# Two more weight places, one row slot fewer, halved attention maps, and loads placed three blocks behind

## The chip, the cores and the metric

The kernel runs on one core of one Trainium2 chip. The metric is the device time of one execution in microseconds (us), lower is better. All numbers are fp32; a "block" of weights is 128 partitions x 2048 values, 1.05 MB.

## What is computed

A trunk of two layers over 256 tokens of width 1024. The part of the reference that matters here, cut to its core:

```python
def reference(x, p, ...):
    h = layer_norm(x, ln_in_g, ln_in_b)
    for i in range(DEPTH):                                   # 2 layers
        mix = token_mixers(h, w_in[i], w_out[i], ...)        # differential attention + indexed sparse attention
        h = layer_norm(ALPHA * h + mix, ln1_g[i], ln1_b[i])
        r = ALPHA * h + peer_ffn(h, peer_wq[i], peer_subkeys[i], peer_u[i], peer_v[i])
        gate = sigmoid(r @ ple_wg[i] + ple_bg[i])
        h = layer_norm(r + gate * (p[i] @ ple_wp[i]), ln2_g[i], ln2_b[i])

def peer_ffn(h, w_q, sub_keys, u_tab, v_tab):                # tables of 16384 experts x 1024
    q = (h @ w_q).reshape(T, 8, 2, 128)                      # 8 heads, 2 halves
    s = einsum('thcd,hckd->thck', q, sub_keys)
    s1, i1 = top_k(s[:, :, 0], 16); s2, i2 = top_k(s[:, :, 1], 16)
    best, pos = top_k((s1[..., :, None] + s2[..., None, :]).reshape(T, 8, 256), 16)
    eidx = take_along_axis(i1[..., :, None] * 128 + i2[..., None, :], pos)   # 8 x 16 experts a token
    act = gelu(einsum('thkd,td->thk', u_tab[eidx], h))
    return einsum('thk,thkd->td', softmax(best) * act, v_tab[eidx])
```

## The kernel before

**Work.** The tokens go in two tiles of 128. Each pair of layer and tile is a run, 0 to 3: runs 0 and 1 are the tiles of the first layer, 2 and 3 those of the second. A run has a *mix* part (projections, both attentions, output projection, first norm, the queries `pq`, the key scores `ps`, and the choice of 128 experts a token) and a *close* part (gate, embedding, second norm). For every run 128 gathers follow: gather k fetches for each of the 128 tokens one expert's row of u and v (2048 values, 1.05 MB in all) from HBM.

**Phases and pairs.** After a start-up the program has four phases. Phase k takes the 128 gathers of run k-1, two at a time, in 64 pairs, and between the pairs it does pieces ("parts") of the mix of run k and of the close of run k-2. Which part stands at which pair on TensorE (PE), ScalarE (ACT) and VectorE (DVE) is written out by hand in `START_*`, `FIRST_PLAN`, `PROJECT_PLAN`, `ATTEND_PLAN`, `CLOSE_PLAN` and their last-phase variants; `make_plan` lays them out. A pair is: two dot products on DVE (L1303, row times token), gelu and two diagonal matrices on ACT (L829, L832, L835), and 2 x 8 small matmuls on PE that add gate times v into the accumulator (L1663; L1658 in the last phase). I write (2,14) for pair 14 of phase 2. Parts named A, B, C with a group number are the choice of experts on DVE: A is the top 16 of each half, B the top 16 of the 256 sums, C the look-up of the indices; `A2b` is group 2, second head.

**Buffers and queues.** Rows land in a ring of `RING` slots. GpSimd (POOL) issues gather k when PE has finished gather k - `RING` (L622, semaphore `slot_done`). The first gathers also wait for some slots that hold weight blocks during the start-up (`EARLY`, `EARLY_SLOTS`). Weight blocks go through a `store` of `PLACES` places. SyncE (SP) issues the loads strictly in the order in which PE uses them (L571), and each load waits for the last use of the block that its place held before. `KEPT_BLOCKS` are blocks that the second tile of a layer needs too: they stay in their places from the first tile's use to the second's. The place of each load is chosen when the program is built, in `count_uses`:

```python
at = min((a for a in range(PLACES) if run is not CLOSE[2] or a not in HELD_LATE), key=lambda a: free[a])
```

that is, the place whose block was done with longest ago.

## Time and profile before

| | |
|---|---|
| median of 3 runs | 1598.83 us (1597.42 to 1599.74) |
| the profiled execution's own time | 1597.55 us, span 1595.8 us |
| busy share of the span | PE 76%, DVE 66%, ACT 42%, POOL 36% |
| moved by DMA | 648.45 MB, mean 406 GB/s |
| of these the gathers (software queue) | 536.90 MB |
| of these the SP and ACT loads | 109.76 MB and 0.34 MB |

The profiled execution is 1.3 us under the median. The rates in GB/s are read against the rate that the DMA engines hold when they have work all the time, which the windows show as 421.

### The profile page before, as it was taken

How to read it: one execution, taken by the hardware profiler on the slowest of the kernel's cores; microseconds unless marked ns; L12 is line 12 of the kernel's file. 1: busy time of each engine (PE TensorE's matmuls, PEld its weight loads, DVE VectorE, ACT ScalarE, POOL GpSimd, SP SyncE). 2: the span in 40 equal slices, each digit the busy share in tenths (PEclk: the TensorE clock that was granted, in tenths of full speed). 3: DMA queues.
4: the chain of work that ended last, by engine and by line, in shares of the span. 5: the costliest groups of instructions: out<-in, count | busy, mean ns of one | idle time of the engine just before them, and what ended most of it. 6: DMA issues, size and time to landing. Idle time of an engine off the chain costs nothing.

```text
span 1595.8 us, 22703 instructions
## 1 busy us (share of the span) xinstructions
PE 1213.1 (76%) x8234; PEld 603.9 (38%) x8234; DVE 1045.3 (66%) x2636; ACT 668.6 (42%) x2027; POOL 580.9 (36%) x518
## 2 busy tenths in 40 slices
PE   9999868787868689786895977978798768444556
PEld 9686423333532266231551335524255223000112
DVE  3467997745778664654688684575578958644555
ACT  2323445723344435363344532536344534323444
POOL 0013443443333323343344332334443434544441
PEclk9999989898888899797997978999899876555557
DMA  9869999999999999999999999999999999999996
GB/s 384 360 250 396 396 421 420 421 421 420 421 420 421 417 396 421 421 420 421 421 421 421 421 417 370 420 421 420 422 420 419 420 421 420 422 421 421 421 421 248
DMA packets 91344, 648.45 MB, mean 406 GB/s; under 512 B 10144, under 2 KB 11616, under 8 KB 13152
## 3 DMA queue, kind: packets, MB, share of 16 engines
q0 software_dynamic: 74016, 536.90, 81.3%
q1 hardware_dynamic: 16704, 109.76, 16.8%
q8 instruction: 65, 1.06, 0.3%
q10 hardware_dynamic: 512, 0.34, 0.1%
q14 instruction: 47, 0.39, 0.1%
HBM read 645.91 MB, written 1.05 MB: 405 GB/s over the span
## 4 chain that ended last, share of the span: by engine, by line
DMA 45%; PE 30%; DVE 14%; ACT 7%; issue 3%; POOL 2%; SPq 0%; ACTq 0%; DVEq 0%; POOLq 0%
DMA rows<-uv_dram,rows_of 39%; PE bank L1343 10%; PE acc L1663 7%; DVE rows L1303 7%; PE bank L1361 5%; DMA store<-wmix_dram 4%; POOL rows L622 2%; ACT dg L835 1%; PE acc L1658 1%; ACT L832 1%; ACT ex L748 1%; PE bank L1614 1%; DMA rows<-wmix_dram 1%; ACT gel L832 1%; DMA store<-wclose_dram 1%
## 5 line engine op out<-in xcount | busy, mean ns | idle before, releaser
L622 POOL DMA_INDIRECT rows<-uv_dram,rows_of x510 | 576.7, 1131 | 985.9 <-PE acc L1663 661.3
L1303 DVE CUSTOM_DVE_ANT_0 rows<-rows,hb 128x1024 f32<-128x1024 f32 x384 | 463.9, 1224 | 313.1 <-DMA rows<-uv_dram,rows_of 310.6
L1663 PE MATMUL acc<-rows,dg 64*64 64x512 f32 x3072 | 453.1, 701 | 198.0 <-ACT dg L835 196.2
L832 ACT ACTIVATE gel<-dots 128x1 f32<-128x1 f32 x512 | 102.7, 201 | 630.1 <-DVE dots L1303 628.7
L1663 PEld LDWEIGHTS acc<-rows,dg 64*64 64x64 f32 x3072 | 102.0, 145 | 459.7 <-ACT dg L835 369.3
L1343 PE MATMUL bank<-xT,store 128*128 128x128 f32 x1888 | 235.1, 286 | 15.7 <-DMA store<-wmix_dram 10.4
L1343 PEld LDWEIGHTS bank<-xT,store 128*128 128x128 f32 x1888 | 225.5, 200 | 55.5 <-issue 41.9
L1303 DVE CUSTOM_DVE_ANT_0 rows<-rows,store 128x1024 f32<-128x1024 f32 x128 | 155.5, 1224 | 119.3 <-DMA rows<-uv_dram,rows_of 118.7
L1658 PE MATMUL acc<-rows,dg 128*32 128x256 f32 x1024 | 119.7, 565 | 133.3 <-ACT dg L835 132.8
L835 ACT ACTIVATE dg<-dg,gel 128x64 f32<-128x64 f32 (+1 forms) x512 | 174.7, 341 | 48.4 <-ACT gel L832 1.5
L1361 PE MATMUL bank<-store,xT 128*128 128x512 f32 x352 | 166.3, 618 | 17.2 <-DMA store<-wmix_dram 14.4
L829 ACT ACTIVATE dg<-fixed,g_of 128x64 f32<-128x64 f32 (+1 forms) x512 | 143.5, 329 | 1.4 <-ACT probsT L648 0.3
L1658 PEld LDWEIGHTS acc<-rows,dg 128*32 128x32 f32 x1024 | 25.9, 132 | 222.9 <-ACT dg L835 212.5
L1361 PEld LDWEIGHTS bank<-store,xT 128*128 128x128 f32 x352 | 66.3, 196 | 110.4 <-issue 94.0
L832 ACT ACT_TABLE_LOAD x51 | 65.4, 1283 | 0.9
L648 ACT ACTIVATE probsT<-bank 128x512 f32<-128x512 f32 (+1 forms) x59 | 30.7, 545 | 42.4 <-PE bank L1343 32.6
L1303 DVE DVE_READ_ACCUMULATOR2_ANT dots<- 128x1 f32 x512 | 42.1, 82 | 0.0
L648 ACT ACTIVATE qT<-bank 128x512 f32<-128x512 f32 (+1 forms) x18 | 9.9, 550 | 59.7 <-PE bank L1343 49.8
L1489 PE MATMUL bank<-prm,fixed 64*128 64x256 f32 x96 | 27.5, 433 | 0.0
L777 ACT ACT_TABLE_LOAD x20 | 25.7, 1283 | 0.4
L1253 DVE TENSOR_TENSOR ex<-ex,i16f 128x512 f32<-128x512 f32 (+1 forms) x38 | 22.6, 594 | 1.3
L1256 DVE TENSOR_REDUCE sel<-ex 128x32 f32<-128x512 f32 (+1 forms) x38 | 22.4, 588 | 1.3
(230 smaller groups left out, 1016.2 us busy)
## 6 DMA issues: line engine op xcount, KB each, us to landing
store<-wmix_dram SPq DMA_DIRECT2D x78, 1024.0 KB, 9.7
store<-wclose_dram SPq DMA_DIRECT2D x15, 1024.0 KB, 10.4
rows<-uv_dram,rows_of POOLq DMA_INDIRECT x510, 16.0
rows<-wmix_dram SPq DMA_DIRECT2D x5, 1024.0 KB, 14.8
rows<-prm_dram SPq DMA_DIRECT2D x2, 1024.0 KB, 19.1
store<-wmix_dram SPq DMA_DIRECT2D x2, 512.0 KB, 9.1
res<-x_dram SPq DMA_DIRECT2D x1, 512.0 KB, 3.7
rows<-wmix_dram SPq DMA_DIRECT2D x1, 512.0 KB, 7.4
```

What stands on the lines that cost most here:

```text
L622: pool.indirect_dma_start(out=rows[:, slot, :], out_offset=None, in_=uv_d[phase // TILES], in_offset=bass.IndirectOffsetOnAxis(ap=rows_of[ ...
L648: ins = A(out, src, func)
L777: A(gexp[:, 0:gs], gexp[:, 0:gs], ACT.Exp).then_inc(gexp_ready, 1)
L829: A(dg[:, s + j, 0:w], one, ACT.Identity, scale=g_of[:, phase % 2, col:col + 1]).then_inc(diag_ready, 1)
L832: A(gel[:, s + j:s + j + 1], dots[:, s + j:s + j + 1], ACT.Gelu).then_inc(gelu_done, 1)
L835: A(dg[:, s + j, 0:w], dg[:, s + j, 0:w], ACT.Identity, scale=gel[:, s + j:s + j + 1]).then_inc(dg_ready, 1)
L1303: V.tensor_tensor_reduce(out=rows[:, s, 0:D], in0=rows[:, s, 0:D], in1=tokens, scale=1.0, scalar=0.0, op0=ALU.mult, op1=ALU.add, accum_out ...
L1343: ins = MM(bk[:, T * at:T * at + T], w[:, T * c:T * c + T], src[:, c, :], start=(c == 0), stop=(c == KC - 1))
L1361: ins = MM(bk[:], xT[:, 2 * q + c, :], w[:, 512 * c:512 * c + 512], start=(q == 0 and c == 0 and extra is None), stop=(q == 3 and c == 1), ...
L1489: ins = MM(bk[:, QCOLS * j:QCOLS * j + QCOLS], chooser(first + i // 2, 2 * (i % 2) + j), prm[:], start=True, stop=True)
L1658: ins = MM(quarters(acc, c)[BT * k:BT * k + BT, :], dg[:, s, 0:BT], rows[:, s, D + 256 * k:D + 256 * k + 256], start=False, stop=False, sk ...
L1663: ins = MM(acc[HT * j:HT * j + HT, 512 * r:512 * r + 512], dg[at, s, :], rows[at, s, D + 512 * j:D + 512 * j + 512], start=False, stop=Fal ...
```

## The change

- The store grows from 10 to 12 places, the ring shrinks from 8 to 7 slots.
- A ninth block, that of `pq0a`, joins `KEPT_BLOCKS`: runs 1 and 3 don't load it again. SP issues 99 block loads in place of 101.
- A load takes the place freed third last before its use (`AHEAD = 3`), not the one freed longest ago; run 0 keeps the old rule.
- Four, not six, of run 0's blocks sit in row slots at the start (`EARLY`); `dk0` and `dk1` sit in the store and are lent to run 1 (`LENT`), which now uses them in phase 1.
- To pay for the store, `ex` (attention maps, key scores) and `probsT` (transposed maps, queries) are halved to 4 maps and 8 blocks (`HELD = 4`). For the second tile the second half of the heads therefore waits until the first is done: `exps1` for `wts0`, `sexp1` for `spt0`, `spt1` for `spv0`, `ps3` and `ps4` for the C step of the groups two before.
- The plans are written out anew around it; parts behind the mix move some pairs later.

```diff
-PLACES = 10
+PLACES = 12
+HELD = 4
-RING = 8
+RING = 7
...
 FIRST_PLAN = [
-    ("pq2a", 0, None, None), ("pq2b", 1, 2, None), ("pq3a", 2, None, None), ("ps2", 3, 4, None), ("pq3b", 4, 5, None),
-    ("pq4a", 5, None, None), ("ps3", 6, 7, None), ("pq4b", 7, 8, None), ("ps4", 9, 10, None),
+    ("pq2a", 1, None, None), ("pq2b", 2, 3, None), ("ps2", 4, 5, None), ("pq3a", 5, None, None), ("pq3b", 7, 8, None),
+    ("ps3", 8, 9, None), ("pq4a", 10, None, None), ("pq4b", 11, 12, None), ("ps4", 13, 14, None),
...
 SINGLY_FIRST = [
-    ("T", 9, 10, None), ("par", 9, 10, None), ("sq0", 11, None, None), ("iw", 13, 14, None), ("sq1", 13, 14, None),
+    ("dk0", 3, None, None), ("dk1", 9, 10, None), ("T", 13, 14, None), ("par", 13, 14, None), ("sq0", 15, None, None),
+    ("iw", 17, 18, None), ("sq1", 17, 18, None),
 ]
+def behind_mix(row):
+    part, *pairs = row
+    late = [p for p in pairs if p is not None]
+    if part[:2] in ("sp", "gb", "mT", "mi", "me") or min(late) < 37:
+        return row
+    return (part, *(None if p is None else p + (2 if p < 54 else 1 if p < 62 else 0) for p in pairs))
...
 def attend_first(p):
-    return p + max(0, min(6, 6 - (p - 50) // 3))
+    return p + max(0, min(8, 8 - (p - 50) // 3))
...
-EARLY = [(U_IQ, U_IQ + 1), (U_IK,)] + [tuple(units_of(part)) for part in ("dq0", "dq1", "dk0", "dk1")]
-EARLY_SLOTS = (3, 2, 4, 5, 6, 7)
-KEPT_BLOCKS = [(U_SK, U_SK + 1)] + [tuple(units_of(part)) for part in ("pq1a", "pq2a", "pq2b", "pq3a", "pq3b", "pq4a", "pq4b")]
+EARLY = [(U_IQ, U_IQ + 1), (U_IK,)] + [tuple(units_of(part)) for part in ("dq0", "dq1")]
+EARLY_SLOTS = (3, 2, 4, 5)
+LENT = [tuple(units_of(part)) for part in ("dk0", "dk1")]
+KEPT_BLOCKS = [(U_SK, U_SK + 1)] + [tuple(units_of(part)) for part in ("pq0a", "pq1a", "pq2a", "pq2b", "pq3a", "pq3b", "pq4a", "pq4b")]
+AHEAD = 3
...
-                at = min((a for a in range(PLACES) if run is not CLOSE[2] or a not in HELD_LATE), key=lambda a: free[a])
-                assert free[at] < i
+                if run is CLOSE[2] and not late:
+                    late = tuple(sorted(range(PLACES), key=lambda a: free[a])[:3])
+                open_to = sorted((a for a in range(PLACES) if free[a] < i and a not in late), key=lambda a: free[a])
+                at = open_to[0] if run is MIX[0] else open_to[max(0, len(open_to) - AHEAD)]
...
                 if part in ("exps0", "exps1"):
                     half = int(part[4])
                     act.wait_ge(dmax_ready, n + n // 2 + 1 + half * tile)
+                    if half and tile:
+                        act.wait_ge(dw_ready, DIFF_HEADS * n + DIFF_HEADS // 2)
...
-                    take(run, part[:3], lists[:, 2 * h0:2 * h0 + 2 * nh, :].rearrange("p c t -> p (c t)"), slice(0, 2 * nh * T))
+                    if part in ("ps3", "ps4"):
+                        act.wait_ge(*((rows_picked, len(GROUPS) * n + g - 1) if n < LAST else (chosen_ready, g - 1)))
+                    take(run, part[:3], lists[:, halves_of(h0, nh), :].rearrange("p c t -> p (c t)"), slice(0, 2 * nh * T))
```

Where the change moves instructions, at three places.

PE, from the last matmuls of the start-up into phase 1. `bank<-res,rows` are run 1's projections from blocks in row slots (`res` holds its transposed tokens), `acc<-rows,dg` the two gathers of a pair. Before:

```order
L1639 MATMUL acc<-hb,fixed 64x512 x4
L1527 MATMUL bank<-store,probsT 128x128 x2
L1343 MATMUL bank<-res,rows 128x128 x48
L1343 MATMUL bank<-xT,store 128x128 x16
L1663 MATMUL acc<-rows,dg 64x512 x8
```

Now:

```order
L1682 MATMUL acc<-hb,fixed 64x512 x4
L1570 MATMUL bank<-store,probsT 128x128 x2
L1383 MATMUL bank<-res,rows 128x128 x16
L1706 MATMUL acc<-rows,dg 64x512 x8
L1383 MATMUL bank<-xT,store 128x128 x16
L1706 MATMUL acc<-rows,dg 64x512 x8
L1383 MATMUL bank<-xT,store 128x128 x16
L1706 MATMUL acc<-rows,dg 64x512 x8
L1383 MATMUL bank<-res,store 128x128 x16
```

In rows as printed x16 is one block. Two of three blocks of run 1 (`dk0`, `dk1`) and the block of `pq2a` have moved from ahead of the first pair to behind it; the first stands at pair 3 now.

PE again, from the end of phase 1 into phase 2 (`acc<-hb,fixed` is `init`, which opens the accumulator of phase 2; `bank<-store,probsT` is a `ps` part). Before:

```order
L1527 MATMUL bank<-store,probsT 128x128 x4
L1663 MATMUL acc<-rows,dg 64x512 x40
L1639 MATMUL acc<-hb,fixed 64x512 x4
L1333 MATMUL bank<-fixed,res 128x128 x8
```

Now:

```order
L1383 MATMUL bank<-xT,store 128x128 x16
L1706 MATMUL acc<-rows,dg 64x512 x16
L1682 MATMUL acc<-hb,fixed 64x512 x4
L1570 MATMUL bank<-store,probsT 128x128 x4
L1373 MATMUL bank<-fixed,res 128x128 x8
```

`ps4` of run 1 stood five pairs ahead of the turn and stands behind it now; the choice of run 1's experts is packed more closely around the turn.

SP, the loads of the last two runs (`wclose` blocks, then `wmix` blocks of run 3). Before:

```order
L571 DMA store<-wclose_dram 128x2048 x4
L571 DMA store<-wmix_dram 128x2048
L571 DMA store<-wmix_dram 128x1024
L571 DMA store<-wmix_dram 128x2048 x17
L592 DMA store<-fixed_dram 128x664
```

Now:

```order
L600 DMA store<-wclose_dram 128x2048 x4
L600 DMA store<-wmix_dram 128x2048
L600 DMA store<-wmix_dram 128x1024
L600 DMA store<-wmix_dram 128x2048 x16
L621 DMA store<-fixed_dram 128x664
```

One full block fewer; the same holds for run 1. What each load waits for follows from `count_uses` and the plans. For the loads around the projections of runs 2 and 3 it gives (used at, part; waits for the last use at, part):

```
run 3 before: (3,14) dq0 <- (3,13) idx   (3,15) dq1 <- (3,13) idx   (3,16) dk0 <- (3,14) dq0   (3,17) dk1 <- (3,15) dq1
run 3 now:    (3,14) dq0 <- (3,5) g1b    (3,15) dq1 <- (3,13) idx   (3,16) dk0 <- (3,13) idx   (3,17) dk1 <- (3,14) dq0
run 2 before: (2,14) dq0 <- (1,56) ps3   (2,14) dq1 <- (1,58) pq4a  (2,15) dk0 <- (1,58) pq4b  (2,15) dk1 <- (2,1) ple
run 2 now:    (2,14) dq0 <- (2,5) g1b    (2,14) dq1 <- (2,13) idx   (2,15) dk0 <- (2,13) idx   (2,15) dk1 <- (2,14) dq0
run 1 before: (1,11) sq0 <- mix1b of the start-up   (1,13) sq1 <- pq0a of the start-up   (1,22) sk0 <- (1,11) sq0
run 1 now:    (1,15) sq0 <- mix1b of the start-up   (1,17) sq1 <- (1,3) dk0              (1,24) sk0 <- (1,9) dk1
```

By the same count the loads up to pair 13 of phase 2 are 55 before and 47 now; one of the eight is the load that is dropped, so seven move to behind that pair.

## Rows read from the trace of the kernel before

**Rows 1.** The page: what DMA moved.

```profile
DMA packets 91344, 648.45 MB, mean 406 GB/s; under 512 B 10144, under 2 KB 11616, under 8 KB 13152
```

**Rows 2.** Windows: busy of each engine, granted clock, DMA share, GB/s.

```profile
70.00:108.00 38.00, 36.56 (x234) 27.47 (x233) 15.30 (x54) 6.74 (x14) 4.20 (x5) 1.00 0.53 184
108.00:140.00 32.00, 32.00 (x279) 26.06 (x278) 21.74 (x75) 13.90 (x37) 11.12 (x12) 1.00 0.98 385
160.00:170.00 10.00, 8.65 (x69) 4.11 (x71) 9.72 (x19) 6.77 (x17) 5.99 (x4) 1.00 0.90 320
200.00:540.00 340.00, 258.16 (x1552) 116.08 (x1552) 238.56 (x614) 151.16 (x446) 125.42 (x113) 0.89 1.01 421
540.00:580.00 40.00, 25.58 (x148) 10.72 (x140) 38.80 (x102) 17.06 (x48) 11.91 (x11) 0.71 1.00 398
...
940.00:970.00 30.00, 18.44 (x124) 11.88 (x121) 25.66 (x61) 12.16 (x37) 8.51 (x7) 0.73 1.01 412
970.00:975.00 5.00, 5.00 (x37) 4.04 (x37) 2.47 (x4) 0.00 (x0) 0.00 (x0) 0.73 0.34 121
```

**Rows 3.** DMA issues: KB of one, median us from issue to landing.

```profile
store<-wmix_dram SPq DMA_DIRECT2D x78, 1024.0 KB, 9.7
...
rows<-uv_dram,rows_of POOLq DMA_INDIRECT x510, 16.0
```

**Rows 4.** Timeline, 100 to 126 us: start, us, engine, line; POOL, then PE.

```profile
102.58 1.07 POOL L622 DMA_INDIRECT rows<-uv_dram,rows_of  x1 [102.13 <-DVE rows_of L1177]
...
115.66 0.93 POOL L622 DMA_INDIRECT rows<-uv_dram,rows_of  x1 [2.64 <-PE bank L1343]
...
124.36 0.94 POOL L622 DMA_INDIRECT rows<-uv_dram,rows_of  x1 [4.20 <-PE acc L1663]
...
108.08 10.88 PE L1343 MATMUL bank<-res,rows 128*128 128x128 f32 x96
...
122.46 1.95 PE L1663 MATMUL acc<-rows,dg 64*64 64x512 f32 x16
```

**Rows 5.** Timeline, 955 to 976 us, PE, SP and POOL.

```profile
957.47 1.95 PE L1663 MATMUL acc<-rows,dg 64*64 64x512 f32 x16
967.40 6.31 PE L1343 MATMUL bank<-xT,store 128*128 128x128 f32 x32 [7.98 <-DMA store<-wmix_dram]
...
957.57 16.50 SPq L571 DMA_DIRECT2D store<-wmix_dram  x3
...
975.04 0.94 POOL L622 DMA_INDIRECT rows<-uv_dram,rows_of  x1 [12.96 <-PE acc L1663]
```

**Rows 6.** Gathers by window (145:165, 540:575, 1380:1480), us to landing.

```profile
DMA to landing us min/median/max: 7.7/8.8/9.4
...
DMA to landing us min/median/max: 7.8/9.9/16.6
...
DMA to landing us min/median/max: 16.0/16.5/17.7
```

**Rows 7.** DVE timeline: an A, a B and a C step, each to what follows it.

```profile
545.65 0.48 DVE L893 MAX8 v<-ex 128x8 f32<-128x128 f32 x2
...
548.75 1.28 DVE L857 BATCH_NORM_STATS2 stats<-res 128x6 f32<-128x512 f32 x2
...
554.17 0.42 DVE L1239 TENSOR_TENSOR sc<-v 128x256 f32<-128x256 f32 x1
...
557.14 1.23 DVE L1303 CUSTOM_DVE_ANT_0 rows<-rows,hb 128x1024 f32<-128x1024 f32 x1
...
566.04 0.18 DVE L1260 TENSOR_TENSOR gexp<-best 128x32 f32<-128x32 f32 x1
...
568.84 1.22 DVE L1303 CUSTOM_DVE_ANT_0 rows<-rows,hb 128x1024 f32<-128x1024 f32 x1
```

**Rows 8.** POOL timeline, the last gathers (L622) and half gathers (L633).

```profile
1561.85 1.20 POOL L622 DMA_INDIRECT rows<-uv_dram,rows_of  x1 [1.28 <-PE acc L1658]
1569.38 1.12 POOL L633 DMA_INDIRECT rows<-uv_dram,late_of  x1 [6.34 <-PE acc L1658]
```

More of the change, by code:

```diff
@@ L159, in loads_of @@
     if run is MIX[1]:
-        blocks = [b for b in blocks if b not in EARLY]
+        blocks = [b for b in blocks if b not in EARLY + LENT]
     return [b for b in blocks if not (run.stage == "mix" and run.tile and b in KEPT_BLOCKS)]
@@ L222 @@
               (f"zgate{_d}", 0, 0, None), (f"zblend{_d}", None, None, 0), (f"zsum{_d}", 0, None, None), (f"znorm{_d}", None, 0, 0)]
-START_PE = ("wake T idx dq0 dq1 dk0 dk1 iw ds0 ix sq0 sq1 dv0 dv1 dpt sk0 dpv sk1 ss0 sv0 sv1 mT0 mix0a spt0 spt1 mix1p spv mix1a mT1 "
-            "T1+ mix0b mix1b idxa+ h1T pq0a ps0 idxb+ dq0+ pq1a init ps1 dq1+ dk0+ dk1+").split()
+START_PE = ("wake T idx dq0 dq1 dk0 dk1 iw ds0 ix sq0 sq1 dv0 dv1 dpt sk0 dpv sk1 ss0 sv0 sv1 mT0 mix0a spt0 spt1 mix1p spv0 spv1 mix1a mT1 "
+            "T1+ mix0b mix1b idxa+ h1T pq0a ps0 idxb+ dq0+ pq1a init ps1 dq1+").split()
 START_ACT = ("embed0 T par idx dq1 dk1 iw ix exps0 exps1 sq1 dv1 dpt dpv sk1 rms sexp0 sexp1 sv1 mT0 embed1 spt0 spt1 mT1 T1+ n1a "
@@ L272, in make_plan @@
         plan[e][0] = [(0, p.rstrip("+"), MIX[p[-1] == "+"]) for p in parts]
-    plan["ACT"][1].append((1, "dk1", MIX[1]))
     def lay(phase, rows, run, moved=int):
@@ L350, in count_uses @@
     last, end = last_reads(), sum(1 for _ in pe_order())
-    uses, free = [0] * PLACES, [-1] * PLACES
+    uses, free, late = [0] * PLACES, [-1] * PLACES, ()
     for i, (part, run) in enumerate(pe_order()):
@@ L746, in part_of @@
                     act.wait_ge(smax_ready, n + n // 2 + 1 + half * tile)
+                    if half and tile:
+                        act.wait_ge(*full_at(run, "spt1"))
                     for i in range(4 * half, 4 * half + 4):
-                        A(ex[:, i, 0:run.keys], sc[:, i, 0:run.keys], ACT.Exp, bias=snmx[:, i:i + 1], scale=SCALE,
+                        A(map_of(run, i), sc[:, i, 0:run.keys], ACT.Exp, bias=snmx[:, i:i + 1], scale=SCALE,
                           accum_out=sden[:, i:i + 1]).then_inc(sexp_ready, 1)
@@ L751, in part_of @@
                     for name in banks_of(run, part):
[L752 removed]
+                        take(run, name, quarter(probsT, int(name[3]) % 2))
                 if part == "rms":
@@ L811, in spread_out @@
                 for half, name in enumerate(banks_of(run, f"hx{c}")):
-                    take(run, name, hx[:, c, 512 * half:512 * half + 512])
+                    take(run, name, hx_of(c)[:, 512 * half:512 * half + 512])
                 for name in banks_of(run, f"hx{c}"):
@@ L820, in pair_of @@
                 P = PAIRS * phase + p
-                s = 2 * P % RING
+                slots = [(2 * P + j) % RING for j in range(2)]
                 w, one = (HT, ident64) if phase < LAST else (BT, ident32)
@@ L992, in part_of @@
                     ins.then_inc(iscore_ready, 1)
-                if part == "wts0":
-                    dve.wait_ge(lamexp_ready, n + 1)
-                    V.tensor_tensor(lamw[:, 4:5], lamw[:, 3:4], lamw[:, 2:3], ALU.subtract).then_inc(L.sem, L.one())
+                if part in ("wts0", "wts1"):
+                    half = int(part[3])
+                    if half == 0:
+                        dve.wait_ge(lamexp_ready, n + 1)
+                        V.tensor_tensor(lamw[:, 4:5], lamw[:, 3:4], lamw[:, 2:3], ALU.subtract).then_inc(L.sem, L.one())
+                        settle()
+                        V.tensor_scalar(lamw[:, 5:6], lamw[:, 4:5], -LAM_INIT[run.layer], None, ALU.add).then_inc(L.sem, L.one())
+                    maps = slice(4 * half, 4 * half + 4)
+                    dve.wait_ge(dexp_ready, 8 * n + 4 * half + 4)
+                    V.reciprocal(rden[:, maps], den[:, maps]).then_inc(L.sem, L.one())
@@ L1002, in part_of @@
                     settle()
-                    for hd in range(DIFF_HEADS):
-                        V.tensor_scalar(ex[:, 2 * hd + 1, 0:nk], ex[:, 2 * hd + 1, 0:nk], nmx[:, 2 * hd + 1:2 * hd + 2],
-                                        None, ALU.mult).then_inc(L.sem, L.one())
-                if part == "wts1":
-                    settle()
-                    for hd in range(DIFF_HEADS):
-                        V.scalar_tensor_tensor(sc[:, hd, 0:nk], ex[:, 2 * hd, 0:nk], rden[:, 2 * hd:2 * hd + 1],
-                                               ex[:, 2 * hd + 1, 0:nk], ALU.mult, ALU.add).then_inc(dw_ready, 1)
+                    for hd in (2 * half, 2 * half + 1):
+                        V.scalar_tensor_tensor(sc[:, hd, 0:nk], map_of(run, 2 * hd), rden[:, 2 * hd:2 * hd + 1],
+                                               map_of(run, 2 * hd + 1), ALU.mult, ALU.add).then_inc(dw_ready, 1)
```

84 lines of the change are left out of this document (48 added, 36 removed), and 28 rows, old and new, of tables (ATTEND_PLAN, FIRST_PLAN).

## The prediction

> **What bounds the kernel now.** I began with the page's DMA line and then cut the span into windows. The page says that 648.45 MB move in 1595.8 us [rows 1]. The windows say at which rate: for 340 us on end in the middle, and in every stretch that isn't named below, the DMA engines hold 421 GB/s with a busy share of 1.01, while no compute engine is full [rows 2]. So I take 421 GB/s as the rate of full DMA engines. 648.45 MB at 421 GB/s are 1540 us; the span is 1596. The kernel is bound by DMA, and only two things can move it: the bytes, and the about 56 us in which the engines are not full. A block or a gather of 1.0486 MB costs 1.0486 / 421 = 2.49 us.
>
> Where the 56 us lie follows from the rates of the windows; a window loses its length times (421 - rate) / 421. 70 to 108 us at 184 GB/s loses 21.4 us, 108 to 140 at 385 loses 2.7, 160 to 170 at 320 loses 2.4, 540 to 580 at 398 loses 2.2, 940 to 970 at 412 loses 0.6, and 970 to 975 at 121 loses 3.6 [rows 2]. What is left is the first 20 us and the last 18, where nothing but first loads or last arithmetic runs.
>
> Then I read what ended the waits in those windows. At 70 to 108 us every place of the store is full, PE is busy (36.6 of 38 us), and gathers can't start before the first indices at 102.1 us [rows 2, 4]. At 108 to 140, gathers 5 to 7 wait for PE to use up the weight blocks that sit in their slots, and gather 8 waits for the first pair on PE, which comes only at 122.5 us, behind 10.9 us of projections of run 1 [rows 4]. At 160 to 170 and 540 to 580 DVE is full (9.7 of 10 us and 38.8 of 40): dot products and the choice of experts take longer than two gathers, and no weight load fills the gap [rows 2]. At 970 it is a chain: PE wants `dq0` at 959.4 us, its load could only be issued at 957.6 us since both free places were in use by `idx`, PE stands for 7.98 us, no slot comes free, and POOL stands for 12.96 us [rows 5].
>
> **The change part by part.**
>
> *Two loads fewer.* 2 x 2.49 us = -5.0 us. They are issued inside phases 1 and 3 where DMA is full, so they count whole. This term does not depend on anything else.
> The Trainium skill, "DMA: Bandwidth & Descriptors", section "Where 436 GB/s comes from", says that the HBM side binds a core at about 358 GB/s; by that figure two blocks would be worth 5.9 us. This trace doesn't agree, since it holds 421.
>
> *Three places in rotation, not two, in phase 3.* By the count in the section on the change, `dq0` then waits for `g1b` at (3,5) and not for `idx`, and the loads after it have about two pairs each to land, where a landing takes 9.7 us in the median [rows 3] and a pair takes at least its two gathers, 5.0 us. The stand of 7.98 us has nothing left that ends late. What is late next is DVE, which is nearly full there too, so I leave 0.2 us: of 0.6 + 3.6 us I take -4.0. Bounds: 0 (another load is late in its place) to -4.2.
>
> *The start.* The hole of 21.4 us is PE's work ahead of the first indices, and that work is unchanged, so it stays. It gets 2.5 us bigger: the load of `sq1` (run 1), which went out in it once `pq0a` was used, waits now for `dk0` at (1,3). Against it stand the 2.7 + 2.4 us behind it. The row at 108.08 holds three blocks; two of them are moved, 2/3 x 10.88 = 7.3 us, and `pq2a` with them. The first pair on PE comes up to 7 us earlier (DVE's first dots are ready about 115 us, so not 11), gather 6 no longer waits for a block, and the two lent places bring loads at pairs 3 and 9, just where DMA now runs short. I take -4.0 of these 5.1 us, together -1.5 us. Bounds: +2.5 (nothing regained) to -2.6 (all of it).
>
> *One slot fewer.* With DMA full and gathers alone, a row lands 16.5 us after its issue [rows 6], although the engines need 2.49 us for it: most of it is queueing, and a slot less only shortens it by one gather, to about 14 us. It costs nothing there. It costs where the queue is short: 8.8 us to landing at 145 to 165 and 9.9 us at 540 to 575 [rows 6], 7.7 us at the shortest: three gathers' time. There a missing row can be an empty queue, at most one gather's 2.49 us for each such place. I count three places (145 to 170, the turn from phase 1 to 2, that from 2 to 3). 0 to 7.5 us; I take +1.5, nearer to nothing, because in two of them DVE is the one that is late (19 of 20 us) and the loads of `dk0`, `dk1` now fill one of them.
>
> *The turn from phase 1 to 2.* The change packs the choice for run 1 into pairs 54 to (2,14), 25 pairs in place of 29. A step of A takes 548.75 - 545.65 = 3.10 us, B 557.14 - 554.17 = 2.97, half a C for two heads 568.84 - 566.04 = 2.80 [rows 7]. 8 A + 8 B + 6 half Cs at 2.80 + 4 for one head at about 1.9 (my estimate from the row of 2.80, with half the elements) make 73 us; with the blends and the norm of the close, about 8 us, and 25 pairs of two dots at 1.22, DVE needs about 142 us less what neighbours overlap, say 140. DMA needs 25 x 2 x 2.49 = 124.5 us and eight loads, some 19 us: 144 us. DMA stays the longer one, by little, and in pairs 6 to 13 of phase 2, which have no loads, DVE is the longer one: two As, two Bs and two half Cs, the blends, the norm and 16 dots are about 43 us by the same prices, against 8 x 4.98 = 40 of gathers; before, one half C fewer, 40 against 40. The loss of 2.2 us grows to about 3.2: +1.0. Bounds 0 to +4.
>
> *The seven loads moved behind (2,13).* They cost no bytes, and DMA is full wherever loads are in flight. A block takes PE 10.88 / 3 = 3.6 us and a pair's gathers 1.95 [rows 4]; counted so, the loads from `dq1` on have 7 to 11 us between the place's release and their use, against a landing of 9.7 [rows 3]. PE will stand for 1 to 3 us at some of them; with three loads and some gathers under way the engines have work meanwhile. I cost it at nothing, with the late loads below as what happens if not.
> The Trainium skill, "DMA: Bandwidth & Descriptors", section "Rules for kernel authors", has it the other way: issue the DMA early and wait late. By that rule loads placed three blocks behind lose against loads placed ten behind. The row at 967.40 agrees where only two places rotate [rows 5]; for three no row shows it. I carry it as a rival.
>
> *The serial halves.* `exps1` now waits for `wts0`, `sexp1` for `spt0`, and so on. They add two tiny DVE instructions a run and one wait each on ACT, behind which the gelu of the next pair stands. All lie some 12 pairs ahead of what needs them (the first indices of run 1 are ready at (1,58), needed near (1,60)). I cost them at nothing; if ACT stood for 3 us in each of the three runs with a full queue of rows, DMA's queue of 14 us would cover it.
>
> *The end.* Gather 509 waits for gather 502, which is done when POOL issues at 1561.85; with seven slots it waits for 503, whose matmuls end about 1569, when POOL issued the next one [rows 8]. Five issues then follow each other from 1569 on, the last one 1.2 us later than now. +0.7 us, bounds 0 to +2.5.
>
> Sum: -5.0 - 4.0 - 1.5 + 1.5 + 1.0 + 0.7 = -7.3 us. The profiled execution took 1597.55 us, so its like would take 1590.25; it lies 1.28 us under the median of 1598.83, and against the median the forecast is **1591.5 us**.
>
> **The rivals.**
>
> *The slot eats the holes (no change).* The ring costs its full 7.5 us in the three places and the start regains nothing but what it loses: -5.0 - 4.0 + 0 + 7.5 + 1.0 + 0.7 = +0.2, 1599 us. For it: in two of these places a row's landing is 8.8 to 9.9 us, as short as it gets. Against it: a queue that is short because DVE is late isn't what holds DVE.
>
> *Loads come too late (no change).* In pairs 14 to 21 of phases 2 and 3 PE stands for weights as at 959.4. Each stand like that one is worth its 3.6 us; two of them in place of one and a gain of nothing elsewhere give 1591.5 + 7.2 = 1598.7 us. For it: the 7 to 11 us above against 9.7. Against it: at 970 there was one load for PE to wait on and no gather; with a third place the next load is under way in the meantime.
>
> *The time left free stays empty (slower).* One mechanism: the seven loads filled DMA while DVE chose run 1's experts; if gathers can't move up into their 7 x 2.49 = 17.4 us because DVE, not DMA, sets the pace from (1,54) to (2,13), they are idle time, and the loads come on top later: 1598.8 - 5.0 - 4.0 + 17.4 = 1607 us. It makes the kernel slower as soon as 12 of the 17.4 us stay empty. For it: DVE's 140 us against 144. Against it: 200 to 540 us holds 421 GB/s with DVE at 238.6 of 340 us [rows 2], and the last part of it is the same choice.
>
> *The loads fill everything (faster still).* The start regains all, the turn loses nothing more, the ring nothing: -5.0 - 4.2 - 2.6 - 2.8 = 1584 us.
>
> **How the numbers follow.** The bound below which I call it no change is 0.2%, 3.2 us (1595.6 to 1602.0). Chances: forecast 0.48 (1586.5 to 1595.6), still faster 0.10, slot 0.14, late loads 0.11, slower 0.17. Faster 0.58, same 0.25, slower 0.17. The range reaches from 1585.5 to 1602: it leaves out half of the case of 1584 and most of that of 1607.
>
> **What would show it.** Right: DMA in all 646.35 MB; the rate at 421 from 110 us on; PE's first `acc` matmul near 115 us; no PE wait on `store` over 4 us near (3,14) and no POOL wait of 13 us; landings of about 14 us in the last phase. Wrong: windows with under 400 GB/s between (1,54) and (2,13) and DVE full in them (the slower rival); PE waits for `store<-wmix_dram` in sum above the present ones in phases 2 and 3 (late loads); holes at 145 to 170 us bigger than 2.4 us (slot).

## The result and the profile after

The changed kernel takes 1607.0 us in the median of five runs (1603.4 to 1608.1), the kernel before 1597.7 (1596.0 to 1599.7). The ratio is 1.0055, 95% interval 1.0044 to 1.0066: it is 8.8 us slower, where 7.3 us faster was forecast. The profiled execution's span is 1606.3 us, 10.5 above that of before. In the runs further down one execution of `before_ahead3` took 2731.6 us; it is left out of that kernel's numbers.

The page, DMA line and the issues of the gathers, as in [rows 1, 3]:

```profile
DMA packets 91056, 646.35 MB, mean 402 GB/s; under 512 B 10112, under 2 KB 11584, under 8 KB 13120
...
rows<-uv_dram,rows_of POOLq DMA_INDIRECT x510, 12.9
```

The bytes fell by the 2.1 MB that were forecast, so all of the 10.5 us, and another 5.0 for the bytes saved, are time in which the DMA engines were not full. Where it lies, the windows say. First those of [rows 2], then four more (columns as there):

```profile
70.00:108.00 38.00, 36.55 (x226) 27.61 (x224) 14.65 (x51) 6.25 (x14) 3.19 (x3) 1.00 0.42 153
108.00:140.00 32.00, 28.89 (x233) 19.47 (x232) 24.82 (x78) 16.09 (x43) 13.22 (x13) 0.95 1.01 409
160.00:170.00 10.00, 9.94 (x88) 7.14 (x81) 9.66 (x20) 6.72 (x17) 5.32 (x5) 1.00 1.02 421
200.00:540.00 340.00, 262.24 (x1616) 123.47 (x1612) 251.35 (x648) 152.72 (x453) 127.80 (x116) 0.89 0.99 408
540.00:580.00 40.00, 30.00 (x208) 17.86 (x212) 31.24 (x79) 16.51 (x47) 12.21 (x10) 0.80 0.94 365
940.00:970.00 30.00, 22.98 (x145) 10.51 (x142) 29.07 (x86) 12.89 (x40) 10.53 (x10) 0.74 1.01 421
970.00:975.00 5.00, 5.00 (x48) 4.01 (x48) 4.93 (x9) 4.26 (x9) 2.67 (x2) 1.00 1.01 418
240.00:262.00 22.00, 14.97 (x103) 11.36 (x104) 21.18 (x51) 8.02 (x21) 4.58 (x4) 0.84 0.86 350
1240.00:1272.00 32.00, 24.13 (x176) 8.54 (x176) 30.86 (x93) 16.61 (x46) 10.34 (x10) 0.89 0.87 330
1100.00:1120.00 20.00, 17.09 (x124) 8.96 (x124) 9.97 (x17) 12.80 (x41) 8.89 (x8) 0.91 0.95 373
...
484.00:500.00 16.00, 13.00 (x44) 5.21 (x48) 15.35 (x52) 5.19 (x15) 1.87 (x2) 0.77 0.89 347
```

By the prediction's measure, length times (421 - rate) / 421, the start (the first three windows) loses 24.2 + 0.9 + 0 = 25.1 us, before 21.4 + 2.7 + 2.4 = 26.5 [rows 2]: 1.4 us gained. The stand at 970 us is gone: 940 to 975 loses nothing, before 4.2. But three stretches that were full before (420 or 421 GB/s) are not: 200 to 540 us loses 340 x 13 / 421 = 10.5 us (of them 3.7 at 240 to 262, 2.8 at 484 to 500 and, at 409 GB/s, 2.9 at 300 to 400), 1240 to 1272 loses 32 x 91 / 421 = 6.9, 1100 to 1120 loses 2.3; and the turn, 540 to 580, loses 5.3 in place of 2.2. Together: -5.0 - 1.4 - 4.2 + 10.5 + 6.9 + 2.3 + 3.1 = +12.2 us against 10.5 measured; the last 18 us of the span, in which 97 GB/s moved where 56 did before, lose 18 x 41 / 421 = 1.8 less.

PE's waits, the sum over the run (waiting line <- releaser: us in total, times, longest), changed kernel:

```profile
PE bank L1657 <- DMA qT<-pT_dram: 8.1, 1, 8.1
PE bank L1383 <- DVE sc L1005: 7.3, 2, 6.1
...
PE bank L1383 <- DMA store<-wmix_dram: 3.2, 3, 2.4
```

and of the kernel before, the two rows in which it waits for weights of the mixing runs:

```profile
PE bank L1361 <- DMA store<-wmix_dram: 14.4, 11, 2.4
PE bank L1343 <- DMA store<-wmix_dram: 10.4, 3, 8.0
```

PE now hardly waits for the weights of the mixing runs: 3.2 us, and 0.5 in the other row, for 24.8. That already speaks against late loads as the cause. It waits for VectorE instead, and once for `pT`, the embedding's input. The dearest place is pair 59 of phase 3. Timeline of the changed kernel, 1231 to 1245 us:

```profile
1233.31 0.44 PE L1580 MATMUL bank<-chosen,fixed 128*32 128x8 f32 x32
...
1233.83 0.17 DVE L1137 CAST rows_of<-bank 128x16 uint32<-128x16 f32 x1 [6.00 <-PE bank L1580]
...
1240.43 1.22 DVE L1343 CUSTOM_DVE_ANT_0 rows<-rows,hb 128x1024 f32<-128x1024 f32 x1
...
1242.38 3.53 PE L1706 MATMUL acc<-rows,dg 64*64 64x512 f32 x16 [4.86 <-ACT dg L872]
...
1244.67 0.94 POOL L651 DMA_INDIRECT rows<-uv_dram,rows_of  x1 [9.55 <-PE acc L1706]
```

Read it down: VectorE comes to `perm1` in its pair 59 and stands 6.00 us, because PE's part of `perm1` now lies in PE's pair 59 too (before in 57, two pairs ahead). Two choice steps, `A2a` and `A2b`, follow in the same pair (before one each in 57 and 58), 3.1 us each [rows 7], and only then the dot product at 1240.43. PE waits 4.86 us for its gate (`dg`), and GpSimd 9.55 us for the slot that PE frees. Seven gathers are at most 7 x 2.49 = 17.4 us of work for the DMA engines when the last is issued; the 330 GB/s at 1240 to 1272 us say that here they ran out.

### The profile page after: what moved, and what is told of

The parts are those of the page before. It is cut to its first block, busy times and chain, and to the rows that moved or that the text cites. A ratio compares the mean times of both kernels' runs of the same rounds, so it can differ in the third digit from the quotient of the medians.

```text
span 1606.3 us, 22713 instructions
## 1 busy us (share of the span) xinstructions
PE 1219.7 (76%) x8234; PEld 608.9 (38%) x8234; DVE 1047.4 (65%) x2644; ACT 665.1 (41%) x2024; POOL 582.8 (36%) x518
## 4 chain that ended last, share of the span: by engine, by line
DMA 38%; PE 34%; DVE 17%; ACT 6%; issue 2%; POOL 1%; SPq 0%; ACTq 0%; DVEq 0%; POOLq 0%
DMA rows<-uv_dram,rows_of 35%; PE bank L1383 11%; PE acc L1706 10%; DVE rows L1343 8%; PE bank L1401 7%; POOL rows L651 1%; PE acc L1701 1%; DMA store<-wmix_dram 1%; DMA qT<-pT_dram 1%; ACT dg L872 1%; PE bank L1657 1%; PE bank L1394 1%; ACT L869 1%; DVE i L933 1%; DVE i L942 1%
## 5 line engine op out<-in xcount | busy, mean ns | idle before, releaser
L1383 PE MATMUL bank<-xT,store 128*128 128x128 f32 x1952 | 244.2, 286 | 12.7 <-DVE sc L1005 7.3
L1383 PEld LDWEIGHTS bank<-xT,store 128*128 128x128 f32 x1952 | 233.8, 200 | 52.1 <-issue 34.1
L1401 PE MATMUL bank<-store,xT 128*128 128x512 f32 x352 | 171.5, 634 | 0.6 <-DMA store<-wmix_dram 0.5
L677 ACT ACTIVATE val<-bank 128x512 f32<-128x512 f32 x16 | 9.4, 593 | 35.9 <-PE bank L1401 21.3
L1532 PEld LDWEIGHTS bank<-prm,fixed 64*128 64x128 f32 x96 | 19.2, 210 | 11.7 <-issue 8.9
## 6 DMA issues: line engine op xcount, KB each, us to landing
rows<-uv_dram,rows_of POOLq DMA_INDIRECT x510, 12.9
```

The lines of the kernel that those rows point to most:

```text
L677: ins = A(out, src, func)
L1383: ins = MM(bk[:, T * at:T * at + T], w[:, T * c:T * c + T], src[:, c, :], start=(c == 0), stop=(c == KC - 1))
L1401: ins = MM(bk[:], xT[:, 2 * q + c, :], w[:, 512 * c:512 * c + 512], start=(q == 0 and c == 0 and extra is None), stop=(q == 3 and c == 1), ...
L1532: ins = MM(bk[:, QCOLS * j:QCOLS * j + QCOLS], chooser(first + i // 2, 2 * (i % 2) + j), prm[:], start=True, stop=True)
```

## The experiments

All are compared with the kernel before on the same chip, five rounds each. The effect of an edit is the difference of two ratios times 1597.7 us; an interval of a ratio is about 0.0009 to 0.0014 either way, so such an effect is good to some 2 to 3 us, and the difference of two effects to some 3 to 4. "Waits as 7" means that GpSimd waits as with seven slots while the buffer has eight. Passing places are those that no kept block holds: two before, three now.

| kernel | slots / places | median us | ratio | 95% interval |
|---|---|---|---|---|
| changed kernel | 7 / 12 | 1607.0 | 1.0055 | 1.0044 to 1.0066 |
| before_gate7 | 8 (waits as 7) / 10 | 1604.1 | 1.0038 | 1.0025 to 1.0051 |
| before_ahead3 | 8 / 10 | 1597.4 | 0.9997 | 0.9988 to 1.0006 |
| after_oldest | 7 / 12 | 1609.7 | 1.0069 | 1.0054 to 1.0083 |
| after_ring8 | 8 / 11 | 1602.9 | 1.0031 | 1.0019 to 1.0043 |
| after_store10 | 8 / 10 | 1602.8 | 1.0042 | 1.0028 to 1.0056 |
| after_perm | 7 / 12 | 1600.2 | 1.0025 | 1.0015 to 1.0034 |
| after_ple | 7 / 12 | 1609.6 | 1.0085 | 1.0071 to 1.0099 |
| after_ring8_fix | 8 / 11 | 1598.6 | 1.0010 | 1.0001 to 1.0019 |
| store10_perm | 8 / 10 | 1601.4 | 1.0029 | 1.0019 to 1.0039 |
| ring8_nine | 8 / 11 | 1595.2 | 0.9984 | 0.9975 to 0.9993 |
| ring8_perm_shift | 8 / 11 | 1597.9 | 1.0009 | 1.0000 to 1.0018 |
| before_gate6 | 8 (waits as 6) / 10 | 1627.1 | 1.0194 | 1.0180 to 1.0207 |
| nine_gate7 | 8 (waits as 7) / 11 | 1604.9 | 1.0036 | 1.0024 to 1.0049 |
| after_perm_shift | 7 / 12 | 1598.8 | 1.0004 | 0.9994 to 1.0013 |
| store10_whole | 8 / 10 | 1599.9 | 1.0008 | 0.9999 to 1.0017 |

Four theories stood against each other: the slot, the new pairs of the parts (with the halves), the late loads, and time that moved loads leave free, which is the last two together.

**The slot alone.** In the kernel before:

```diff
-                        if k >= RING:
-                            pool.wait_ge(slot_done, k - RING + 1)
+                        if k >= RING - 1:
+                            pool.wait_ge(slot_done, k - RING + 2)
```

> The kernel before with one edit: GpSimd issues gather k only when gather k-7 is used up, as with seven slots; buffers, plan and loads stay. It computes the same. If the missing slot makes the new holes (the recorded term of +1.5 us, bounds 0 to 7.5), this kernel loses most of the 15 us of holes that the changed kernel has more: +8 us or more, about 1606. If the new places of the parts or the loads placed three blocks behind make them, it stays within 0 to +3 us of before, 1598 to 1601.

It costs 0.0038 x 1597.7 = 6.1 us: under the 8 of the first theory and over the 3 of the others. Windows of this kernel, then of the kernel before:

```profile
113.00:175.00 62.00, 56.95 (x460) 38.71 (x462) 51.78 (x153) 29.98 (x87) 22.61 (x22) 0.97 0.93 370
450.00:480.00 30.00, 23.69 (x160) 12.09 (x160) 27.07 (x86) 11.76 (x35) 10.19 (x10) 0.78 0.98 402
545.00:590.00 45.00, 31.13 (x206) 16.51 (x207) 38.59 (x94) 17.88 (x52) 13.67 (x13) 0.81 0.99 386
1020.00:1045.00 25.00, 20.81 (x124) 13.39 (x125) 17.51 (x39) 15.02 (x40) 7.08 (x6) 0.89 1.00 399
```

```profile
113.00:175.00 62.00, 56.79 (x458) 37.67 (x456) 51.18 (x151) 29.24 (x84) 23.94 (x24) 0.96 0.98 388
450.00:480.00 30.00, 20.42 (x152) 10.51 (x144) 25.46 (x81) 10.73 (x31) 11.20 (x11) 0.84 1.01 421
545.00:590.00 45.00, 34.01 (x228) 18.82 (x232) 37.32 (x92) 18.25 (x53) 13.45 (x12) 0.80 1.00 395
1020.00:1045.00 25.00, 20.97 (x116) 9.64 (x112) 15.93 (x37) 15.86 (x45) 8.50 (x8) 1.00 1.01 420
```

The loss is small and in several places (here 2.7, 1.4, 1.0 and 1.2 us), two of these full before. How a full place comes to lose, the fourth shows. Timeline of the kernel with seven:

```profile
1018.50 1.23 DVE L1303 CUSTOM_DVE_ANT_0 rows<-rows,hb 128x1024 f32<-128x1024 f32 x1 [2.50 <-DMA rows<-uv_dram,rows_of]
...
1019.95 1.41 DVE L968 SCALAR_TENSOR_TENSOR sc<-fixed,bank 128x256 f32<-128x256 f32 x4
...
1020.75 6.09 PE L1343 MATMUL bank<-xT,store 128*128 128x128 f32 x32 [5.47 <-DVE sc L968]
...
1028.16 1.85 POOL L622 DMA_INDIRECT rows<-uv_dram,rows_of  x1 [11.35 <-PE acc L1663]
```

and the same steps in the kernel before:

```profile
1011.49 1.41 DVE L968 SCALAR_TENSOR_TENSOR sc<-fixed,bank 128x256 f32<-128x256 f32 x4
...
1014.74 3.84 PE L1343 MATMUL bank<-xT,store 128*128 128x128 f32 x32
1019.90 0.94 POOL L622 DMA_INDIRECT rows<-uv_dram,rows_of  x1 [3.52 <-PE acc L1663]
```

Before, VectorE computes the scores `sc` at 1011.49, 3.3 us ahead of the matmuls that need their bank (1014.74). With one row fewer ahead it comes to `sc` only at 1019.95, right behind a row for which it waited 2.50 us; PE, ready at 1015.3, stands 5.47, and GpSimd stands 11.35 for PE. At this place the slot is not only cover for a stand, it keeps apart engines that otherwise meet.

**Six slots.** The same edit with `k - RING + 3`.

> The kernel before with GpSimd's wait two gathers further back, as with six slots. It computes the same. The first slot cost 6.3 us. If a slot costs where a pair is long, each further slot opens more such places: 16 to 30 us over before, 1614 to 1628, with landings of gathers in the last phase near 11.5 us. If it costs one gather's 2.5 us at each of the same two or three places, 1610 to 1611.

1.0194, +31 us, at the upper end of what was expected (1627.1 us for 1614 to 1628): the first slot costs 6, the second 25. Landings of gathers are shorter, as forecast (median 11.3 us of all 510, 16.0 with eight; 11.6 from 1380 to 1480 us), and it helps nothing.

**The slot given back.** The changed kernel with eight slots, eleven places and `pq0a` loaded again:

```diff
-PLACES = 12
+PLACES = 11
-RING = 7
+RING = 8
```

> The changed kernel with a ring of eight slots, eleven places and the block of pq0a loaded again in runs 1 and 3 (two loads, +5.0 us of bytes at 421 GB/s); plan, halves and the three-behind rule stay. It computes the same. If the missing slot makes the holes, they shrink by 8 us or more and the time is 1604 or less in spite of the two loads. If the slot costs nothing beyond its bounds, the holes stay and the two loads add to the changed kernel: 1609 to 1612.

1.0031, 3.8 us less in spite of 5.0 us of loads (by their bytes): with three places passing in both, the slot is worth some 8.8 us in this plan.

**The late loads.** The rule for places of the change on the kernel before, and the old rule on the changed kernel (`at = open_to[0]` for every run):

> The kernel before with the changed kernel's rule for places (three places behind the newest) on its ten places; plan, ring, kept blocks stay. It computes the same. If late loads alone cost (the rivals 'loads come too late' and 'time left free stays empty'), this kernel is 5 to 12 us slower than before, with PE waits on store above 4 us at pairs 0 to 2 of phases 2 and 3 and less in flight from pair 54 on. If they cost only together with the new plan, it is within 2 us of before (it may even gain up to 4 us at 970 us, where two places rotate).

> The changed kernel with one edit: every load takes the place that came free first (as before), with all twelve places; plan, halves, ring of seven stay. It computes the same. If the loads three blocks behind make the holes, it comes to 1591 to 1597 us (the hole of 2.8 us at 492-501 and most of the 5.5 at 551-571 gone, and others with it). If the plan's new places make them, only the hole at 492-501 goes and the holes at 254-268, 1106-1116 and 1242-1270 stay: 1602 to 1606; it may lose up to 4 us more at the start of phase 4's predecessor, since in phase 3 loads then wait for the oldest of three places.

-0.5 us and +2.2 us: neither can be told from nothing, and loads in the old order don't gain. As the cause of the lost 8.8 us the theory falls. But the rule is not without effect at single places, as the windows of the changed kernel with the old rule show:

```profile
484.00:500.00 16.00, 9.36 (x75) 3.95 (x78) 15.42 (x38) 6.62 (x22) 4.33 (x5) 1.00 1.01 418
1240.00:1272.00 32.00, 22.58 (x124) 7.63 (x128) 30.76 (x101) 16.10 (x44) 10.62 (x10) 0.84 0.73 274
```

The first hole closes (418 GB/s for 347, 2.7 us), and the one at `perm1` grows (274 for 330, 4.3 us). In the changed kernel the first is at the turn, where the first close's loads are late:

```profile
474.27 0.33 SPq L600 DMA_DIRECT2D store<-wclose_dram  x1
474.78 0.33 SPq L608 DMA_DIRECT2D qT<-pT_dram  x1
...
487.00 5.81 PE L1657 MATMUL bank<-store,qT 128*128 128x512 f32 x8 [8.12 <-DMA qT<-pT_dram]
...
494.13 0.94 POOL L651 DMA_INDIRECT rows<-uv_dram,rows_of  x1 [13.37 <-PE acc L1706]
```

These five loads alone were put early, with `pT` ahead of them:

```diff
-at = open_to[0] if run is MIX[0] else ...
+at = open_to[0] if run in (MIX[0], CLOSE[0]) else ...
```

> The changed kernel with one edit: the loads of the first close (ple to g1b at pairs 0 to 5 of phase 2) take the places free longest, so that they go out near pair 45 of phase 1, and pT's load is put ahead of them in SP's queue. It computes the same. If their late issue makes the hole at 492-501 us, 2 to 3 us come back: 1604 to 1605, and PE's wait of 8.1 us for pT is gone. If DMA time is only moved (loads early, gathers starved at the VectorE-bound turn), the hole at 551-571 grows by as much and the time stays: 1606 to 1609.

1.0085, 4.8 us slower than the changed kernel, where 1604 to 1609 us was expected. PE's wait of 8.12 us goes away, but the hole doesn't close: with VectorE full (21.07 of 22 us; 17.54 in the changed kernel) it loses 22 x 96 / 421 = 5.0 us, where the changed kernel, at 367 GB/s, loses 2.8:

```profile
487.00:509.00 22.00, 20.88 (x85) 7.86 (x84) 21.07 (x74) 12.66 (x32) 7.37 (x7) 1.00 0.90 325
```

That full VectorE turns the earlier loads into a loss is argued from this window and not tested by itself. The profiled execution of this kernel is also 0.7 us shorter than that of the changed one (spans 1605.6 and 1606.3 us), so this trace can't account for the 4.8 us of the medians. With eight slots the same edit costs nothing (1.0010 and 1.0009, below). Why it costs with seven stays open.

**The plan and the halves, without the store.** The changed kernel with eight slots, ten places, eight blocks kept, as before:

> The changed kernel with the storage of before: ring of eight, ten places, eight blocks kept and two passing (pq0a loaded again in runs 1 and 3). Only the plan, the halves, the two lent blocks and the rule for places of the change are left. It computes the same. If the new plan with its halves costs by itself (hand-offs at pair 59 of phase 3, at 25 of phase 1, the blocks of ple loaded late), it lies 5 to 9 us above before, 1603 to 1607: the 5.1 us that the kernel with eight slots and eleven places lies above before, and up to 4 us for the hole near 970 us that three passing places had closed. If the plan costs nothing and the slot and its consequences are all, it lies within 2 us of before, 1596 to 1600.

1.0042, +6.7 us: the plan, with the halves, the lent blocks and the rule for places, costs by itself. The eleventh place, a third one passing, takes 1.8 us off that (after_ring8, 1.0031), which can't be told from nothing. Then the plan's single steps.

**perm1.** On the changed kernel, `perm1` of run 3 goes to pair 61 on VectorE, and `A2a`, `A2b`, `B2a`, `B2b`, `C2a`, `C2b`, `A3a`, `A3b` to 58 to 65, one each:

> The changed kernel with one edit in the plan of run 3: VectorE takes perm1 at pair 61 (two pairs behind TensorE's part, as it was before the change) and the choice steps A2a to A3b lie one to a pair from 58 on. It computes the same. If the hand-off makes the hole at 1242-1270 us (6.8 us lost there), 4 to 6 us come back: 1601 to 1603. If the ring of seven makes it wherever a pair is long, the hole stays and the time is within 1.5 us of the changed kernel, 1605 to 1608.

1.0025, 4.8 us back (6.9 by the medians). The edit puts back two things at once: the two pairs between PE's and VectorE's `perm1`, and one choice step to a pair. Timeline, then windows of this kernel:

```profile
1237.12 1.01 POOL L655 DMA_INDIRECT rows<-uv_dram,rows_of  x1 [5.48 <-PE acc L1710]
...
1238.40 0.17 DVE L1141 CAST rows_of<-bank 128x16 uint32<-128x16 f32 x1
```

```profile
240.00:262.00 22.00, 15.72 (x116) 11.44 (x120) 21.18 (x50) 8.49 (x22) 3.89 (x4) 0.84 0.92 368
...
1240.00:1272.00 32.00, 22.05 (x200) 8.37 (x196) 30.76 (x93) 18.16 (x53) 13.64 (x13) 0.88 1.01 419
```

VectorE no longer stands at `perm1`, GpSimd's 9.55 became 5.48, and 1240 to 1272 us holds 419 GB/s with VectorE as busy as before the edit (30.8 of 32 us). It was the order, not the load; which of the two steps of the edit did it was not tested. On the storage of before the same edit gives less:

> The kernel of the changed plan on the storage of before (ring of eight, ten places; it took 1602.8), with the one edit of VectorE's perm1 to pair 61 and the choice steps one to a pair. It computes the same. If that hand-off is all that the new plan costs, its 5.4 us over before are gone: 1595 to 1599. If the rest of the plan costs too (halves, run 1 two pairs later), it stays 2 us or more above before: 1600 to 1603.

1.0029: 2.1 us, which can't be told from nothing. By the windows the hole that it closes is there with eight slots too, and smaller: ahead of the edit 1240 to 1272 us loses 32 x 45 / 421 = 3.4 us (376 GB/s in after_store10), with seven slots 6.9. Eight slots seem to hide about half of it.

**ds0.** What is left of the first window above is pair 25 of phase 1, where `C4b0` and `ds0` of run 1 share VectorE's pair, and PE and GpSimd stand (changed kernel):

```profile
250.28 6.44 PE L1383 MATMUL bank<-xT,store 128*128 128x128 f32 x32 [6.08 <-DVE sc L1005]
...
258.04 1.50 POOL L651 DMA_INDIRECT rows<-uv_dram,rows_of  x1 [13.45 <-PE acc L1706]
```

Run 1's attention was put a pair later:

```diff
-    return p + max(0, min(8, 8 - (p - 50) // 3))
+    return p + (9 if p < 37 else max(0, min(8, 8 - (p - 50) // 3)))
```

> The changed kernel (ring of seven, twelve places, nine kept, three passing) with perm1 mended and run 1's attention a pair later. It computes the same. With perm1 alone it took 1600.2 and had a hole of 2.4 us at 254-258. If that hole comes from ds0 sharing VectorE's pair with C4b0, 1 to 2.5 us come back: 1597.5 to 1599.5. If a hole there only moves to another pair, 1599.5 to 1601.

1.0004: another 3.4 us, of which the window shows 22 x 43 / 421 = 2.2: it rises from 368 to 411 GB/s.

```profile
240.00:262.00 22.00, 18.18 (x125) 11.82 (x126) 21.32 (x49) 9.60 (x27) 8.03 (x6) 0.84 1.01 411
```

**The halves.** `store10_perm` with the maps whole again (`HELD = 8`) and without the three waits on ScalarE:

> The changed plan on the storage of before with perm1 mended (1601.4), with attention maps, their transposes and the keys in full buffers again, and without the three waits of ScalarE that the halves need; the order of the parts stays. It computes the same. If these waits are part of the 4.1 us that are left over before, 1598 to 1600. If they are free, as the prediction had it, within 1.2 us of 1601.4.

1.0008 for 1.0029: 3.4 us by the ratios, 1.5 by the medians. The intervals just don't meet, so the halves seem to cost something, and the size is not settled. No trace shows where: from 1095 to 1125 us, in phase 3, the rate is 408 GB/s in store10_perm and 420 in store10_whole, which is 30 x 12 / 421 = 0.9 us; but the profiled execution of store10_whole was the slowest of its eleven (1604.5 us).

**Eight slots and the mended plan.** Three kernels:

> Eight slots, eleven places, pq0a not kept, and three edits in the plan: perm1 of run 3 as in the kernel above, the loads of the first close as in the one above, and run 1's attention from ds0 to merge a pair later, so that it no longer shares VectorE's pair 25 with C4b0. It computes the same. The kernel with eight slots took 1602.9 with holes of 6.6 us at 1238-1270, 3.0 at 489-499, 1.6 at 255-266. If the plan makes these, 6 to 10 us come back: 1593 to 1597, at or under the kernel before. If they only move, it stays at 1600 to 1603.

> As the kernel with eight slots and three plan edits (1598.6), without its edit to the loads of the first close, which alone cost 2.6 us on the changed kernel. Eleven places, pq0a not kept, three passing. It computes the same. If early loads of the first close starve the turn by VectorE, this one is 1595.5 to 1597.5; if the third passing place is worth its 4 us near 970 us too, 1594. If the earlier difference was chance, 1598 to 1599.

> Ring of eight, eleven places, nine blocks kept (two loads fewer than before, -5.0 us) and two passing, with perm1 as above and run 1's attention a pair later; the rule for places is the changed kernel's. It computes the same. If bytes count whole and hand-off and slot are the whole loss, it lies 5 us under before less what two passing places lose near 970 us (before too has two there, 4.1 us): 1592 to 1594, the fastest so far. If the serial halves or the late loads cost beyond that, 1596 to 1599.

The first has the edit for the close's loads as well, the second doesn't; they are the same within their intervals (1.0010, 1.0009). Neither gained the 6 to 10 us that were expected of the first: with eight slots both edits of the plan give 3.5 us (1.0031 to 1.0009), with seven they gave 8.1 (1.0055 to 1.0004). The third keeps nine blocks and lets two places pass: 0.9984, 4.0 us under the second and 2.6 us under the kernel before, the fastest of all. Its 1595.2 us lie between the two ranges that were expected, so part of the 5.0 us of bytes is lost again.

**The slot again, on the fastest version.**

> The fastest version so far (ring of eight, eleven places, nine kept, perm1 and run 1's attention moved; 1595.2) with GpSimd's wait one gather further back, as with seven slots. It computes the same. If the slot costs by itself as on the kernel before (6.3 us), 1600 to 1603. If it cost mainly through the stall at perm1, which is mended here, 1596 to 1598. If slot and the other long pairs of this plan lose together, 1604 or more.

1.0036: 8.3 us for the slot, with `perm1` mended. And against it stands after_perm_shift, the same but with twelve places, so a third one passing: 1.0004, 5.1 us for that place.

But slot, place and hand-offs have no fixed price each. after_perm_shift (seven slots) and ring8_perm_shift (eight) have the same plan and three places passing, and differ else only in the two loads of `pq0a`. They lie 0.8 us apart, so with three places passing the slot is worth 5.0 - 0.8 = 4.2 us, not 8.3. In the same way the third passing place is worth 5.1 us with seven slots and, by ring8_nine, 5.0 - 4.0 = 1.0 with eight. These differences, like the 8.1 and 3.5 us for the edits of the plan, are a little above their own error of some 3.3 us. Where the ring is short, a third place and a looser plan are worth more, and the other way round.

## Why the prediction was wrong

The step that failed is **One slot fewer**, taken at +1.5 us with "It costs nothing there" where DMA is full. The runs show 6.1 us on the plan of before and 8.8 on the new one, in part from stretches that were full. Next to it stand the new pairs of the parts, for which the sum has no term but that of the turn, and **The serial halves**, "I cost them at nothing": plan and halves cost 6.7 us together with eight slots and ten places.

- *One slot fewer.* 6.1 us alone on the kernel before; on the new plan 8.8, and with `perm1` and `ds0` mended 8.3 with two places passing and 4.2 with three. All are well over the +1.5 taken, and two are over the upper bound of 7.5, though not clear of the error. That bound was built from three places where the landing was shortest; the loss lies in full stretches too (450 to 480 and 1020 to 1045 us above). I read the queue's 16.5 us [rows 6] as cover that a stand must first use up, and did not ask which stands lie just under it. In the new plan there are many: `ds0`, the first close, `perm1`. Seven slots also make new stands, as at 1020 us, where VectorE runs into rows that haven't landed. That a landing only shortens to about 14 us was right (14.0 us, last section), and was no measure of the price.
- *The moved parts.* I weighed VectorE's sum of work over 25 pairs and never looked at hand-offs at single pairs. `perm1` two pairs nearer to its maker, with two choice steps in one pair, cost 4.8 us with seven slots; run 1's attention, with `ds0` in the pair of `C4b0`, 3.4 us. Both can be read from the plans of the change.
- *The serial halves.* Hardly nothing: 3.4 us by the ratios, 1.5 by the medians, where the intervals just don't meet.
- *The turn.* +3.1 us by the windows, forecast +1.0 with bounds to +4. The mechanism was VectorE's packed work, and the runs speak for the slot instead: the kernels of the new plan with seven slots hold 363 to 369 GB/s from 540 to 580 us (381 with the old rule for places), and with eight slots and three places passing it is 393 to 398, before 398. So the number lay within the bounds by luck. Window of ring8_perm_shift:

```profile
540.00:580.00 40.00, 31.65 (x236) 21.22 (x236) 28.75 (x63) 14.07 (x45) 13.29 (x11) 0.86 0.99 398
```

- *The start.* -1.4 us by the windows (the hole 2.8 larger, the stretch behind it 4.2 better), forecast -1.5 (2.5 and 4.0): right in mechanism and size. PE's first `acc` matmul came at 116.47 us, forecast near 115.
- *Three places in rotation.* -4.2 us by the windows, forecast -4.0, and the stand at 970 us is gone; in the total 5.1 us by the runs with seven slots, 1.0 to 1.8 with eight.
- *Two loads fewer.* The bytes are as forecast. With eight slots keeping `pq0a` gave 4.0 us net of the passing place that it takes.
- *The seven loads moved.* Nothing in the total, as forecast: on the kernel before the rule for places moved the time by -0.5 us (0.9988 to 1.0006), and the old rule on the changed kernel by +2.2. The Trainium skill, "DMA: Bandwidth & Descriptors", section "Rules for kernel authors", has the DMA issued early and waited for late; in this kernel, whose queue is full of gathers, these two runs show no gain from it.
- *The end.* Forecast +0.7, and not tested by itself. The first dots of pair (4,48) start at 1504.84 us before and at 1515.55 now, 10.7 apart, and the spans are 10.5 apart, so the end costs nothing.

The runs lead from the kernel before to the changed one in two ways. Without the edits of the plan: +6.7 (plan and halves, after_store10) - 1.8 (eleventh place, after_ring8) - 5.0 (bytes) + 8.8 (slot) = +8.7 us. Through the edits: -2.6 (ring8_nine) + 8.3 (slot) - 5.1 (third passing place) + 3.4 (`ds0`) + 4.8 (`perm1`) = +8.8 us. Both end on the measured 8.8 because each step is the difference of two runs in a row; they are no check of each other. What is independent is that the bytes (-5.0, counted) and the halves (+3.4) make -1.6 of the first -2.6, within the error. Within that account the wrong sign of the forecast comes from slot, hand-offs and halves; how they share it depends on the order in which they are taken.

Of the rivals, the slower one gave 1607 us, the measured time, but its mechanism is at most a part. Gathers did move up: the first dots of pair (2,0) start at 474.68 us, before at 491.90, 17.2 us earlier. At pair (2,14) 10.0 us of the lead are left:

```profile
566.18 1.22 DVE L1343 CUSTOM_DVE_ANT_0 rows<-rows,hb 128x1024 f32<-128x1024 f32 x1
```

```profile
576.22 1.22 DVE L1303 CUSTOM_DVE_ANT_0 rows<-rows,hb 128x1024 f32<-128x1024 f32 x1
```

Windows from pair (2,0) to (2,14), of the changed kernel and of the kernel before:

```profile
474.70:566.20 91.50, 62.69 (x312) 23.23 (x311) 75.71 (x209) 41.61 (x108) 29.74 (x26) 0.81 0.96 386
```

```profile
491.90:576.20 84.30, 63.48 (x307) 23.03 (x308) 67.30 (x168) 38.65 (x104) 30.07 (x26) 0.84 1.01 412
```

It loses 91.5 x 35 / 421 = 7.6 us there, for 84.3 x 9 / 421 = 1.8 before: 5.8 us more, under the 12 from which that rival decides. The sign that the prediction named for it is there, though: 484 to 500 us has 347 GB/s with VectorE 15.35 of 16 us busy. With the time that it gave, the rest of the loss (`ds0`, `perm1`, 1100 to 1120 us) came from elsewhere, so its 1607 is luck. "The slot eats the holes" was nearest: it named the slot at 7.5 us, near the 8.8 on this plan, and had nothing for the hand-offs.
